# Decoder trunk on one core: another order of the MLP's outer products, and the sums between its reads placed anew

## The reference, cut to what matters

```python
h = x + (mixed @ w_out)                                # 1088 x 1024 by 1024 x 1024
n2 = rms_norm(h, norm2_g)
y = h + (jnp.square(jax.nn.relu(n2 @ w_up)) @ w_down)  # w_up 1024 x 4096, w_down 4096 x 1024
```

## Time and profile before

| | |
|---|---|
| median of three runs | 2105.36 us (2101.52 to 2110.78) |
| profiled execution, own time | 2111.22 us |
| its span, first to last instruction | 2109.6 us |
| PE busy | 1984.7 us, 94% of the span |
| DVE busy | 1245.8 us, 59% |
| POOL busy | 582.2 us, 28% |
| ACT busy | 615.9 us, 29% |

### The profile page before, as it was taken

The page is one execution under the profiler, slowest core; times in us unless marked ns, Lnnn a source line. Parts: engine busy times, 40 slices in busy tenths (PEclk is TensorE's granted clock), DMA queues, the critical chain, the costliest instruction groups (busy, mean ns, idle before and its releaser), DMA issues.

```text
span 2109.6 us, 39724 instructions
## 1 busy us (share of the span) xinstructions
PE 1984.7 (94%) x15956; PEld 1235.5 (59%) x15956; DVE 1245.8 (59%) x2528; ACT 615.9 (29%) x1428; POOL 582.2 (28%) x715
## 2 busy tenths in 40 slices
PE   8999999898988898989988998999999999999998
PEld 6445656788876774444444444555556564647473
DVE  4375654466654448776656438756566565747473
ACT  5004543333332226666644222101010101101020
POOL 3000000344441002212102013535353535344441
PEclk9999999999997998999999999999999999999999
DMA  7001113101023611000045601111111111111112
GB/s 224 0 0 30 31 25 99 63 5 24 5 52 103 182 52 56 11 6 11 1 135 187 205 1 40 41 40 40 40 40 41 40 41 40 40 40 40 40 41 85
DMA packets 96917, 115.91 MB, mean 55 GB/s; under 512 B 32251, under 2 KB 68028, under 8 KB 96670
## 3 DMA queue, kind: packets, MB, share of 16 engines
q1 hardware_dynamic: 90718, 101.82, 15.4%
q10 hardware_dynamic: 4480, 7.34, 1.2%
q0 software_dynamic: 1536, 4.20, 0.6%
HBM read 104.75 MB, written 12.64 MB: 56 GB/s over the span
## 4 chain that ended last, share of the span: by engine, by line
PE 82%; DVE 9%; ACT 4%; issue 3%; ACTq 0%; DMA 0%; POOL 0%; DVEq 0%; POOLq 0%
PE psum L1578 43%; PE psum L1581 31%; PE psum L2201 2%; DVE arena L3082 2%; PE psum L2085 1%; ACT arena L1443 1%; PE psum L2258 1%; ACT arena L1429 1%; DVE arena L2913 1%; DVE arena L2939 1%; DVE arena L3057 1%; DVE arena L3053 1%; DVE arena L3055 1%; PE psum L1924 0%; PE psum L1643 0%
## 5 line engine op out<-in xcount | busy, mean ns | idle before, releaser
L1578 PE MATMUL psum<-arena 64*64 64x64 f32 (+16 forms) x11020 | 1026.5, 300 | 67.3 <-issue 26.5
L1578 PEld LDWEIGHTS psum<-arena 64*64 64x64 f32 (+6 forms) x11020 | 588.4, 144 | 410.5 <-issue 228.0
L1581 PE MATMUL psum<-arena 128*128 128x272 f32 (+1 forms) x2464 | 763.3, 469 | 19.9 <-DVE arena L3082 16.9
L1581 PEld LDWEIGHTS psum<-arena 128*128 128x128 f32 x2464 | 459.4, 190 | 322.6 <-issue 218.1
L3104 DVE TENSOR_TENSOR arena<-arena,psum 128x512 f32<-128x512 f32 x224 | 154.1, 688 | 237.9 <-PE psum L1581 237.9
L3082 DVE TENSOR_TENSOR arena<-arena,psum 128x272 f32<-128x272 f32 x328 | 142.1, 433 | 70.0 <-PE psum L1581 66.1
L1543 ACT ACTIVATE arena<-psum 128x272 f32<-128x272 f32 x64 | 25.4, 397 | 507.4 <-PE psum L1581 507.4
L1028 POOL TENSOR_TENSOR arena<-arena 128x512 f32<-128x512 f32 x17 | 21.6, 1273 | 359.7 <-DVE arena L2749 359.7
L1093 POOL TENSOR_TENSOR arena<-arena 128x256 f32<-128x256 f32 x56 | 41.8, 746 | 285.0 <-PE psum L1581 285.0
L1429 ACT ACTIVATE arena<-psum 128x512 f32<-128x512 f32 (+1 forms) x148 | 80.5, 596 | 68.7 <-PE psum L2201 60.7
L1022 POOL TENSOR_TENSOR arena<-arena 128x256 f32<-128x256 f32 x82 | 61.9, 755 | 119.9 <-PE psum L1578 119.7
(11 more groups left out here) (325 smaller groups left out, 1999.5 us busy)
## 6 DMA issues: line engine op xcount, KB each, us to landing
arena<-in_w_up_dram SPq DMA_DIRECT2D x7, 2048.0 KB, 8.5
arena<-in_w_down_dram SPq DMA_DIRECT2D x7, 2048.0 KB, 7.8
arena<-in_cache_slc_kv_dram SPq DMA_DIRECT2D x96, 128.0 KB, 2.5
arena<-in_cache_cmp_kv_dram SPq DMA_DIRECT2D x72, 128.0 KB, 3.4
arena<-in_x_prompt_dram SPq DMA_DIRECT2D x16, 512.0 KB, 12.8
arena<-in_cache_cmp_kv_dram ACTq DMA_DIRECT2D x56, 128.0 KB, 3.3
arena<-in_w_in_dram SPq DMA_DIRECT2D x13, 512.0 KB, 3.8
arena<-in_w_in_dram SPq DMA_DIRECT2D x2, 2048.0 KB, 19.1
```

The costliest lines, as they stand in the source:

```text
L1578: return nc.tensor.matmul(out, lhsT, rhs, start=start, stop=stop)
L1581: return nc.tensor.matmul(out, lhsT, rhs, start=start, stop=stop, skip_group_check=True)
```

## The change

The outer order becomes 1, 2, 6, 7, 4, 5, 3. Chain 1's product now goes first into the hidden block of chain 6 (`ONTO`, `BASE`, `ADDED_TO`), so that chain 2 can come second. With it come these moves:

- The sample rows' output product goes between the first and the second pair, DVE's additions for it (`sample_hidden`) too, and the turns of that tile between products of the second pair. Product 6 of the second pair waits for these additions, since it uses their bank. The turn of tile 6 goes behind step 5 of chain 1.
- ACT has two buffers of normed rows. The norm of tile 6 is split (`hidden_scale`, `hidden_out`) around ACT's first copy.
- Row sums of group 0 are made in pieces. `t_row3` is computed from two blocks, by columns as tiles arrive, `t_row2` as `t_row3` plus a block, and their quarters are put behind single reads. POOL makes one block's `inner_rows` (two operations).
- Weight sums leave chains 2, 6, 7 and 4. Four (n = 1, 2) stand in chain 5, and four (n = 3, 4) behind reads of the first down chain.

```diff
-        UP_ORDER = (1, 6, 2, 7, 4, 5, 3)
+        UP_ORDER = (1, 2, 6, 7, 4, 5, 3)
-        ONTO = {1: (1, 1), 6: (1, 2), 2: (1, 1), 7: (2, 2), 4: (2, 1), 3: (1, 2)}
-        BASE = {6: (1, 1), 7: (1, 2), 4: (2, 2)}
+        ONTO = {1: (1, 2), 2: (1, 1), 6: (1, 2), 7: (2, 2), 4: (2, 1), 3: (1, 2)}
+        BASE = {2: (1, 2), 7: (1, 2), 4: (2, 2)}
+        ADDED_TO = {2: 1, 6: 1, 7: 6, 4: 7, 3: 6}
...
+                    if g == 0 and x == 3:
+                        pool.wait_ge(*once("rows_t3"))
+                        v = up_rows(2, 2)
+                        link(plus(right_block(v, 1, 2), right_block(v, 2, 2), right_block(v, 1, 2), ALU.subtract))
+                        plus(right_block(v, 1, 2), right_block(v, 1, 2), right_block(v, 1, 1), ALU.add).then_inc(once("rows_22")[0], 1)
...
                 for p in (1, 6, 5, 4):
                     first_copy(n, p)
+                    if g == 0 and p == 1:
+                        hidden_out(6)
...
+                if z == O0 + 1 and p == 6:
+                    pe.wait_ge(sem("h_ready"), 3)
...
                     if (z - O0, p) in TURNS:
                         turn_normed(*TURNS[z - O0, p])
+                if z == O0:
+                    pe.wait_ge(sem("u_sum"), 2 * z + 1)
+                    for e in range(2 * KT):
+                        ins = out_product(PT, e % 2, e // 2, 0, KT - 1)
+                    ins.then_inc(sem("h_mm"), 1)
             turn_normed(7, 0)
             turn_normed(7, 1)
-            pe.wait_ge(sem("u_sum"), 2 * M0 - 1)
-            for e in range(2 * KT):
-                ins = out_product(PT, e % 2, e // 2, 0, KT - 1)
-            ins.then_inc(sem("h_mm"), 1)
-            turn_normed(6, 0)
-            turn_normed(6, 1)
...
-                    if (n, p) == (0, 2):
-                        turn_normed(PT, 0)
-                        turn_normed(PT, 1)
+                    if (n, p) == (0, 5):
+                        turn_normed(6, 0)
+                        turn_normed(6, 1)
...
+            def rows_t3(cols):
+                return mark(tt(t_row3[:, :, cols], b22[:, :, cols], b12[:, :, cols], ALU.subtract))
+            def rows_t2(r, c):
+                return tt(right_block(t_row2, r, c), right_block(t_row3, r, c), right_block(b11, r, c), ALU.add)
...
+            def first_row_sums(i, p):
+                if i == 2:
+                    if p == 2:
+                        inner_row_sum(1, 7)
+                    elif p == 5:
+                        inner_row_sum(1, 4)
+                    elif p == 1:
+                        rows_t2(1, 1)
...
                     if kind == "down":
                         down_read(n, p)
+                        if i == 0 and p in (1, 2, 6, 5):
+                            down_weight_sum(g, *{1: (3, 0), 2: (3, 1), 6: (4, 0), 5: (4, 1)}[p])
...
+                    if i == 5:
+                        if p in (1, 2, 5, 3):
+                            down_weight_sum(g, *{1: (1, 0), 2: (1, 1), 5: (2, 0), 3: (2, 1)}[p])
+                        else:
+                            inner_row_sum(7 * g + 6, {6: 5, 7: 7, 4: 4}[p])
+                    elif i == UP_ORDER[-1]:
+                        if p in (1, 6, 7, 4):
+                            e_added(g, (1, 6, 7, 4).index(p))
+                    elif g == 0:
+                        first_row_sums(i, p)
+                    elif p in (1, 6, 7):
                         inner_row_sum(up_no(g, i) + 1, {1: 5, 6: 7, 7: 4}[p])
```

More of the change, by code:

```diff
@@ L370, in decode_trunk @@
         t_down = [work(2, 512) for _ in range(4)]
+        t_sb, u2, u3 = (region(37888 + 512 * x, 512) for x in range(3))
         s_two = work(4, 2 * P)
@@ L374, in decode_trunk @@
         wl2 = [work(4, 2, P) for _ in range(2)]
+        s_out_high = region(at[0], 4, 4, P)
+        t_row2 = work(4, HT)
         s_out_low = region(at[0], 4, 4, P)
-        t_row2, t_row3 = work(4, HT), work(4, HT)
-        assert at[0] <= N0
-        at[0] = 37888
-        hn = work(D_MODEL)
-        t_sb, u2 = hn[:, 0:512], hn[:, 512:]
-        u3 = work(512)
+        t_row3 = work(4, HT)
         assert at[0] <= N0 - 512
         at[0] = ARENA
+        m1_sb, m16_sb, m167_sb = (region(at[0] + 512 * x, 512) for x in range(3))
         tl2_even = work(3, 2, QT)
-        s_out_high = region(at[0], 4, 4, P)
         e_at = at[0]
+        hn = [region(e_at + D_MODEL * x, D_MODEL) for x in range(2)]
         e_sum = work(2, HT)
@@ L517, in normed_rows @@
         def normed_rows(t):
-            return hn if t in LATE_NORMED else y[:, PT, :]
+            return hn[normed(t) % 2]
         def turn_bank_of(t, half):
@@ L2439, in up_step @@
                     if g == 0:
-                        pe.wait_ge(*once(TOKENS[i]))
+                        pe.wait_ge(*once("rows_t2_left" if i == 6 else TOKENS[i]))
                     pe.wait_ge(sem("wl2"), c + 1)
+                if p == 6 and g == 0 and i == 6:
+                    pe.wait_ge(*once("rows_t2"))
                 if p in (5, 7, 4):
@@ L3195, in _ @@
-            ins.then_inc(sem("h_ready"), 1)
+            dve.wait_ge(sem("n2_out"), 2 * normed(7) + 2)
+            rows_t3(TILES_78)
+            up_read(0, 2)
+            inner_row_sum(1, 5)
             n2_out(6, 0)
             n2_out(6, 1)
-            dve.wait_ge(sem("n2_out"), 2 * normed(6) + 2)
-            left, right = slice(0, QT), slice(QT, HT)
-            b11, b12, b21, b22 = (up_rows(r, c) for r in (1, 2) for c in (1, 2))
-            link(tt(t_row2[:, :, left], b22[:, :, left], b12[:, :, left], ALU.subtract))
@@ L3212, in _ @@
[L3212 to L3226 removed]
+            up_read(0, 7)
```

177 lines of the change are left out of this document (111 added, 66 removed).

## The result

The changed kernel takes 2086.68 us (median of 7 runs, 2084.46 to 2094.04) against 2108.09 us of the kernel before (7 runs, 2101.52 to 2110.78): a ratio of 0.9908 with a 95% interval of 0.9891 to 0.9925. It is faster by 1%, 6.7 us above the 2080 forecast and inside the range. Its profiled execution took 2089.61 us.

What follows compares the result with a forecast made beforehand. PE's waits in the up chains, for DVE reads standing behind sums, were taken as the loss, 38.5 us in all. 2105.4 less 11.3 (first group) and 14.5 (seven others) gave 2079.6, say 2080 us; range 2071 to 2093.

Steps and rivals of the forecast that it cites:

- Later groups: Up chains of the seven groups after the first: shorter waits in chains 2, 6, 7, 4 and 5, 14.5 us gained.
- The weight sums n = 3 and 4: First down chain: these sums hide behind its reads, where DVE idles 1.10 us, and cost nothing.
- Product 6 of the second pair starts without a wait: Output product: its new wait comes 6.9 us after the sample product and needs 1.7 us of DVE, no cost.
- POOL's sums follow each other: Sign in the up chains: POOL's first weight sums should follow each other at 6.6 us from chain to chain.
- T + 8: Up chains of later groups, T being chain 5's start: the row sum for chain 3's step 4 ends by then.
- rival 2: Later groups' up chains: their waits only move, only group 0's 11.3 us remains, 2094 us; chance 0.10.
- Group 0: Up chains of the first group, DVE mostly the limit: 50.8 us in place of 61.7, 10.9 gained.
- The start of chain 1: First group's first up chain: starts 0.4 us earlier, tile 6's turn gone and the sample tile's moved into the pairs.
- Rival 1: Up chains: DVE sums collide with POOL at their dearest, 1.16 to 1.36 us each in group 0; 2090.5 us, chance 0.14.

Runs made afterwards that it cites:

- the sums back: The changed kernel with each group's eight weight sums put back at their old places, also n = 3 and 4 in chain 5: 2104.69 us.
- the pieces together: The changed kernel with group 0's outer row-sum pieces in runs behind reads 5 and 4, not one behind each read: 2099.39 us.
- one sum later: The changed kernel with weight sum (2, 1) moved from behind step 3 of chain 5 to behind step 5 of chain 3: 2084.10 us.
- two later: The changed kernel with weight sums (2, 1) and (2, 0) moved from chain 5 to behind reads 5 and 2 of chain 3: 2084.28 us.

## Why the prediction was right, and where its sizes were off

**Right, with its numbers.** Later groups: chains 2, 6, 7 and 4 lose 0.16 us (forecast 0.17) and chain 5 0.36 (0.4). The weight sums n = 3 and 4 cost nothing, the down chains lose 0.1 us before and after. Product 6 of the second pair starts without a wait: it is the second half of a row of 16 records of products 7 and 6 (1238.53 to the turn at 1245.40), which are 0.43 us apart throughout. POOL's sums follow each other at 6.57 us (6.6). In group 0 chains 1, 2, 7, 4 and 5 came at 8.18, 7.68, 7.31, 6.89, 7.24 for 8.0, 7.9, 7.0, 6.7, 7.15. The kernels with the sums back and the pieces together show the mechanism: the order of sums between reads, at the same volume on DVE, decides.

**The term that failed: chain 3.** The prediction held that the row sum for the last chain's step 4 "ends by T + 8, in time for that chain". It ended at T + 8.9 (1434.03 less 1425.10). Two things were left out. The row sum stands, with the weight sum (2, 1), ahead of the read of chain 3's step 1, whose bank step 6 wants, so being in time for step 4 was not enough. And both meet POOL's hidden sums, 0.89 us in all; at T + 8.0 the read would have been in time. This is 0.84 us where 0.02 stood, so that a later group gains 1.31 in place of 2.1: 5.5 us for seven. It is rival 2's mechanism, a wait that moves on along DVE's queue, in another place and to less than half of the gain. The kernel with one sum later took 0.51 of it away, the one with two later showed that it moves back and forth.

**Group 0: 9.0 in place of 10.9.** Chain 6 took 8.43 for 7.6. The step priced a sum beside POOL from sums that met operations of 0.73 us, and put POOL's two new operations at 0.3 us for DVE in all (7.6 for 2.45 of reads, four sums at 0.90 and two at 0.63); they are 1.8 and 1.7 us long, and a DVE sum beside one lasts 1.50. With them small, chain 6 is 7.62 and chain 7 has its time too. Chain 3 took 6.97 for 6.45, by the term above. The other sums beside POOL were somewhat cheaper than the 0.90 taken: 0.83 from start to start (1304.52 to 1305.35, 1305.69 to 1306.52).

**The start of chain 1: 0.34 us later, not 0.4 earlier.** Each half of the sample tile's turn costs 0.48 us within the pairs, where about 0.5 was taken for both, and 0.1 is lost at three changes of shape.

**The sum.** 5.5 + 1.9 + 0.7 is 8.1 us too much; 25.8 less that is 17.7, near the 18.2 that the traces give the change. The medians differ by 21.4, with the 15.8 to 23.0 of their interval. So the forecast of 2080 missed by less (6.7) than its sum did (8.1), and that is luck: some 3 us of the measured gain lie outside what was changed, and in the other direction the kernel before stands at 2108.09 where the forecast started from 2105.36.

**Rival 1** had the right cause for much of what is left: without POOL's inner weight sums the kernel is some 10 us faster. But the meetings were not at their dearest: in chains 2, 7 and 4 of group 0 the row sums and pieces of 544 elements beside POOL lasted at most 0.94 us, where the rival needed 1.16 to 1.36.

## What to carry to other kernels

When sums are moved behind other reads of an engine that works in program order, follow its queue up to the first reads of the next stage: each operation there has two deadlines, its own result's and that of the read behind it. Put such a sum where the engine idles before its next read and little is owed behind it; here behind step 3 and not step 5, for 0.15 us of each chain. And where two engines collide, price the meeting by the length of the operation that is met, not by an average of former meetings.
